# Two layer norms taken by token tiles, weight and bias applied with the copies out of PSUM, and a product moved beside the second norm

## What is computed

```python
x = _layernorm(DEEPNORM_ALPHA * x + h, ln_g[i, 0], ln_b[i, 0])      # h: GDN mixer
h = _hier_moe(x, moe_w_group[i], ..., moe_w_down[i])                # 32 experts, hidden 256
x = _layernorm(DEEPNORM_ALPHA * x + h, ln_g[i, 1], ln_b[i, 1])
x = x + jax.nn.sigmoid(x @ pe_w_gate[i]) * (p[i] @ pe_w_proj[i])

def _layernorm(t, g, b):
    mu = jnp.mean(t, axis=-1, keepdims=True)
    var = jnp.mean(jnp.square(t - mu), axis=-1, keepdims=True)
    return (t - mu) * lax.rsqrt(var + LN_EPS) * g + b
```

## Time and profile before

| what | value |
|---|---|
| median of three runs | 1308.56 us |
| profiled execution, its own time | 1311.29 us |
| its span | 1309.8 us |
| busy: PE, DVE, ACT, POOL | 1123.8, 370.3, 363.0, 48.8 us |
| mean granted TensorE clock | 0.907 of full |
| HBM read | 207.91 MB, 160 GB/s over the span |
| chain that ended last | PE 72%, SP queue 10%, DVE 6%, ACT 5%, DMA 4% |

### The profile page before, as it was taken

How to read it: one execution, slowest core, us unless ns; L and a number is a source line. 1 busy time by engine, 2 the same in 40 slices (tenths; PEclk the granted TensorE clock), 3 DMA queues, 4 the chain that set the end, 5 groups by cost and what they waited for, 6 DMA issues and landing times.

```text
span 1309.8 us, 23489 instructions
## 1 busy us (share of the span) xinstructions
PE 1123.8 (86%) x10332; PEld 852.1 (65%) x10332; DVE 370.3 (28%) x879; ACT 363.0 (28%) x902; POOL 48.8 (4%) x55
## 2 busy tenths in 40 slices
PE   6799999999889869767775979999997989996668
PEld 5577777777667654233332868888886877864457
DVE  1455655565442231000003124220002000614310
ACT  2345554655543111000003031120014011225220
POOL 1110010000000000000000000000000000400000
PEclk9799999999989969888886969999998998997559
DMA  5421221122011689999994224434441354430000
GB/s 209 185 100 66 91 75 67 67 92 74 35 66 65 280 367 407 420 421 421 422 421 193 97 100 146 159 111 147 161 160 65 101 189 115 177 129 1 0 1 33
DMA packets 35529, 210.55 MB, mean 161 GB/s; under 512 B 4688, under 2 KB 9168, under 8 KB 11488
## 3 DMA queue, kind: packets, MB, share of 16 engines
q1 hardware_dynamic: 35424, 209.00, 41.6%
HBM read 207.91 MB, written 1.08 MB: 160 GB/s over the span
## 4 chain that ended last, share of the span: by engine, by line
PE 72%; SPq 10%; DVE 6%; ACT 5%; DMA 4%; issue 2%; PEld 0%; PEldq 0%; ACTq 0%; DVEq 0%
PE ps L245 15%; SPq L230 10%; PE ps L397 10%; PE ps L1894 8%; PE ps L1812 4%; PE ps L400 4%; PE ps L698 2%; PE ps L709 2%; DMA arena<-in_wu 2%; PE ps L460 2%; PE ps L2225 2%; PE ps L426 2%; PE ps L445 2%; PE ps L261 1%; PE ps L1375 1%
## 5 line engine op out<-in xcount | busy, mean ns | idle before, releaser
L245 PE MATMUL ps<-slots,xt 128*128 128x256 f32 x640 | 139.1, 379 | 0.7 <-ACT xt L272 0.7
L397 PE MATMUL ps<-xt,slots 128*128 128x256 f32 x512 | 132.5, 407 | 2.0 <-DMA slots<-in_wu 2.0
L245 PEld LDWEIGHTS ps<-slots,xt 128*128 128x128 f32 x640 | 121.4, 190 | 17.8 <-ACT xt L272 1.1
L397 PEld LDWEIGHTS ps<-xt,slots 128*128 128x128 f32 x512 | 99.3, 202 | 26.7 <-issue 10.3
L1894 PE MATMUL ps<-slots,xt 128*128 128x256 f32 x512 | 110.7, 379 | 0.0
L1894 PEld LDWEIGHTS ps<-slots,xt 128*128 128x128 f32 x512 | 97.2, 190 | 13.2
L1375 PE MATMUL ps<-arena 128*32 128x512 f32 x304 | 48.9, 696 | 17.7 <-DMA arena<-in_wu 10.6
L400 PE MATMUL ps<-slots,arena 128*128 128x256 f32 x256 | 63.1, 389 | 0.0
L245 PE MATMUL ps<-slots,yt 128*128 128x256 f32 x256 | 57.8, 390 | 0.9 <-ACT yt L275 0.9
L1812 PE MATMUL ps<-xt,slots 128*128 128x256 f32 x256 | 58.1, 391 | 0.0
L989 DVE SCALAR_TENSOR_TENSOR arena<-arena 128x256 f32<-128x256 f32 x128 | 56.7, 489 | 0.3
(11 more groups left out here) (353 smaller groups left out, 1592.0 us busy)
## 6 DMA issues: line engine op xcount, KB each, us to landing
slots<-in_wu SPq DMA_DIRECT2D x120, 1024.0 KB, 4.9
arena<-in_wu SPq DMA_DIRECT2D x56, 1024.0 KB, 26.5
yt<-in_wu SPq DMA_DIRECT2D x10, 1024.0 KB, 26.2
arena<-bias_rows SPq DMA_DIRECT2D x1, 2048.0 KB, 15.6
arena<-in_xp SPq DMA_DIRECT2D x2, 512.0 KB, 4.4
xt<-in_xt SPq DMA_DIRECT2D x2, 512.0 KB, 9.2
x<-in_x SPq DMA_DIRECT2D x1, 1024.0 KB, 17.1
arena<-in_ln_g SPq DMA_DIRECT2D x2, 512.0 KB, 14.6
```

Source lines behind the costliest of these rows:

```text
L245: q = M.matmul(self.bank(cg, UC, t * UC), lhs[:, h * KT + k, t * P:(t + 1) * P], self.slot(s)[:, k, :], start=(t == 0 and k == 0 and h == ...
L397: q = M.matmul(bank(n, T), self.slots[:, s, k, n * P:(n + 1) * P], self.xt[:, k, :], start=(k == 0), stop=(k == KT - 1))
```

## The change

The change does five things. (1) Both norms go token tile by token tile: statistics, rsqrt, then x becomes (x - mean) * rsqrt in one DVE instruction (`norm_centre`), PE turns that (`norm_tensor`), and weight and bias are applied per feature with the copies out of the banks, four of 128x128 by ACT and four by DVE, from a small array `lnf` with features on the partitions. x itself gets its weight and bias rows afterwards (`norm_rows`). (2) In the first norm, tile 0's transposes stand ahead of the last group of the output projection, and tile 1's between the router's products of the two tiles. (3) At the end, p's product stands right behind the branch, ahead of the second norm's transposes, in banks 0 to 3; the gate projection uses banks 4 to 7. `pt` and `lnf` are loaded at the start of the MoE stage, and slot 4 is refilled ahead of slots 0 to 3. (4) The count `spill_over` of the case without spill is raised by POOL. (5) ACT's dummy Ln activations are replaced by an explicit load of the table set that holds Ln and Exp.

```diff
-        for cg in range(4):
-            self.out_rest(1, cg, 0, KT)
...
         with self.nc.Else():
-            self.nc.tensor.sem_inc(g.spill_over.sem, 1)
+            self.nc.gpsimd.sem_inc(g.spill_over.sem, 1)
+        self.moe_end_tensor(g)
+        self.moe_end_scalar(g)
         self.moe_end_vector(g)
...
     def moe_sync(self, g):
+        SP.dma_start(g.lnf, I["lnf"]).then_inc(*g.loaded.up())
+        SP.dma_start(g.pt[:, :, :], I["pt"]).then_inc(*g.loaded.up())
...
-        SP.wait_ge(*g.normed(1))
+        SP.wait_ge(*g.normed(2))
...
-        for s in range(6):
+        for s in (4, 0, 1, 2, 3, 5):
             self.fill(s, U_PE + s)
     def moe_tensor(self, g):
-        M.wait_ge(*g.normed(1))
-        self.turn_tensor(self.x, KT, [0, 1], g.turned, g.xt_kept)
-        M.wait_ge(*g.xt_kept(4))
-        M.wait_ge(*g.loaded(4))
-        for t in range(NT):
+        for cg in range(3):
+            self.out_rest(1, cg, 0, KT)
+        self.norm_tensor(g, 0, 0, OUT_BANKS[0:2])
+        self.out_rest(1, 3, 0, KT)
+        M.wait_ge(*g.loaded(6))
+        for t in range(NT):
+            M.wait_ge(*g.xt_kept(t + 1))
+            M.wait_ge(*g.xt_kept_v(t + 1))
             for k in range(KT):
                 q = M.matmul(bank(2, NG, t * NG), self.xt[:, k, t * P:(t + 1) * P], g.wr[:, k, :], ...)
+            if t == 0:
+                self.norm_tensor(g, 0, 1, OUT_BANKS[2:4])
...
     def moe_scalar(self, g):
-        A.activation(self.warm[:, 0:1], self.col(3), ACT.Ln)
-        self.norm_scalar(g, g.stats, g.var(1), 0)
-        self.turn_scalar(self.xt, KT, [0, 1], g.turned, g.xt_kept)
+        A.preload_act_table_set("natural_log_exp_and_others")
+        for t in range(NT):
+            self.norm_scalar(g, 0, t)
+            self.norm_kept_scalar(g, 0, t, OUT_BANKS[2 * t])
...
+    def norm_tensor(self, g, row, t, banks):
+        M.wait_ge(*g.centred(2 * row + t + 1))
+        for j in range(2):
+            for k in range(4):
+                q = M.transpose(self.bank(banks[j], P, k * P), self.x[:, t, (4 * j + k) * P:(4 * j + k + 1) * P],
+                                self.c["ident"])
+            q.then_inc(*g.turned.up())
+    def norm_kept_scalar(self, g, row, t, bank):
+        A.wait_ge(*g.loaded(6))
+        A.wait_ge(*g.turned(2 * (2 * row + t) + 1))
+        for k in range(4):
+            q = A.activation(self.xt[:, k, t * P:(t + 1) * P], self.bank(bank, P, k * P), ACT.Identity,
+                             scale=g.lnf[:, row, 0, k:k + 1], bias=g.lnf[:, row, 1, k:k + 1])
+        q.then_inc(*g.xt_kept.up())
+    def norm_kept_vector(self, g, row, t, bank):
+        V.wait_ge(*g.loaded(6))
+        V.wait_ge(*g.turned(2 * (2 * row + t) + 2))
+        for k in range(4, KT):
+            q = V.tensor_scalar(self.xt[:, k, t * P:(t + 1) * P], self.bank(bank, P, (k - 4) * P),
+                                g.lnf[:, row, 0, k:k + 1], g.lnf[:, row, 1, k:k + 1], ALU.mult, ALU.add)
+        q.then_inc(*g.xt_kept_v.up())
+    def norm_stats(self, g, t):    # two bn_stats of 512, one bn_aggr
+    def norm_centre(self, g, row, t):
+        V.wait_ge(*g.var_exp(2 * row + t + 1))
+        V.tensor_scalar(x, x, st[:, t, 12:13], st[:, t, 13:14], ALU.subtract, ALU.mult).then_inc(*g.centred.up())
+    def norm_rows(self, g, row, t):
+        V.wait_ge(*g.loaded(6 + 2 * row))
+        V.wait_ge(*g.turned(2 * (2 * row + t) + 2))
+        V.tensor_tensor(x, x, g.rows[:, 0], ALU.mult).then_inc(*g.step.up())
+        V.wait_ge(*g.step.last())
+        V.tensor_tensor(x, x, g.rows[:, 1], ALU.add).then_inc(*g.normed.up())
...
     def moe_vector(self, g):        # per tile t, behind the two adds of L1497
-        V.wait_ge(*g.x_added(4))
-        self.norm_vector(g, 0, g.var)
+            V.wait_ge(*g.x_added.last())
+            self.norm_stats(g, t)
+            self.norm_centre(g, 0, t)
+            self.norm_kept_vector(g, 0, t, OUT_BANKS[2 * t + 1])
+            self.norm_rows(g, 0, t)
...
+    def moe_end_tensor(self, g):
+        M.wait_ge(*g.loaded(6))
+        M.wait_ge(*self.arrived[4](self.multiplied[4].n + 1))
+        for cg in range(4): ...     # p's product, into banks 0 to 3
+        for t in range(NT):
+            self.norm_tensor(g, 1, t, (4 + 2 * t, 5 + 2 * t))
+        for t in range(NT):
+            M.wait_ge(*g.xt_kept(NT + t + 1))
+            M.wait_ge(*g.xt_kept_v(NT + t + 1))
+    def moe_end_scalar(self, g):
+        self.nc.scalar.preload_act_table_set("natural_log_exp_and_others")
+        for t in range(NT):
+            self.norm_scalar(g, 1, t)
+        for t in range(NT):
+            self.norm_kept_scalar(g, 1, t, 4 + 2 * t)
     def moe_end_vector(self, g):
+        add(0)
+        self.norm_stats(g, 0)
+        add(1)
+        self.norm_centre(g, 1, 0)
+        self.norm_stats(g, 1)
+        self.norm_kept_vector(g, 1, 0, 5)
+        self.norm_centre(g, 1, 1)
+        self.norm_kept_vector(g, 1, 1, 7)
+        for t in range(NT):
+            self.norm_rows(g, 1, t)
...
     def embed_sync(self, g):
-        SP.wait_ge(*self.normed(2))
-        SP.dma_start(g.pt[:, :, :], self.ins["pt"]).then_inc(*g.loaded.up())
     def embed_tensor(self, g):
-        M.wait_ge(*self.normed(2))
-        self.turn_tensor(self.x, KT, [0, 1], g.turned, g.xt_kept)
-        ...                         # p's product, into banks 4 to 7
-        g.projected = self.project(self.xt, 4, 1)
+        g.projected = self.project(self.xt, 4, 1, base=4)
     def embed_scalar(self, g):
-        A.activation(self.warm[:, 2:3], self.col(3), ACT.Ln)
-        self.turn_scalar(self.xt, KT, [0, 1], g.turned, g.xt_kept)
     def embed_vector(self, g):
+            if cg == 0:
+                V.wait_ge(*self.normed(4))
```

More of the change, by code:

```diff
@@ L230, in fill, with project @@
         SP.dma_start(self.slot(slot), self.ins["wu"][unit]).then_inc(*self.arrived[slot].up())
-    def project(self, lhs, units, halves, emptied=None, slots=(0, 1, 2, 3)):
+    def project(self, lhs, units, halves, emptied=None, slots=(0, 1, 2, 3), base=0):
         M, groups, done = self.nc.tensor, 4 // halves, []
@@ L1250, in moe @@
         g.og, g.cr = al("og", [P, D]), al("cr", [P, NT, 1])
+        g.pt, g.lnf = al("pt", [P, 2, T]), al("lnf", [P, 2, 2, KT])
         assert self.top <= ARENA - (NSLOT - 8) * KT * UC
@@ L1443, in moe_scalar @@
             A.activation(g.og[:, 0:512], self.bank(0), ACT.Copy).then_inc(*g.og_a.up())
[L1444 to L1449, removed]
+    def norm_tensor(self, g, row, t, banks):
+        M = self.nc.tensor
+        M.wait_ge(*g.centred(2 * row + t + 1))
[4 more added lines that the diff above has]
+            q.then_inc(*g.turned.up())
@@ L1460, in norm_vector @@
         q.then_inc(*g.step.up())
         V.wait_ge(*g.step.last())
[L1462 to L1470, removed]
-        V.wait_ge(*g.step.last())
-        V.wait_ge(*g.var_exp(row + 1))
@@ L1473, in norm_vector @@
[L1473 to L1476, removed]
+        V.bn_aggr(st[:, t, 12:14], st[:, t, 0:12]).then_inc(*g.var.up())
+    def norm_centre(self, g, row, t):
+        V, st, x = self.nc.vector, g.stats, self.x[:, t]
+        V.wait_ge(*g.var_exp(2 * row + t + 1))
+        V.tensor_scalar(x, x, st[:, t, 12:13], st[:, t, 13:14], ALU.subtract, ALU.mult).then_inc(*g.centred.up())
@@ L1645, in spill_vector @@
             q.then_inc(*g.spill_made.up())
+    def moe_end_tensor(self, g):
+        M, wp = self.nc.tensor, self.flat(4).rearrange("p (f n) -> p f n", f=2)
+        M.wait_ge(*g.loaded(6))
+        M.wait_ge(*self.arrived[4](self.multiplied[4].n + 1))
+        for cg in range(4):
+            for t in range(NT):
+                for f in range(2):
+                    q = M.matmul(self.bank(cg, UC, t * UC), g.pt[:, f, t * P:(t + 1) * P],
+                                 wp[:, f, cg * UC:(cg + 1) * UC], start=(f == 0), stop=(f == 1),
+                                 skip_group_check=True)
+        q.then_inc(*self.multiplied[4].up())
+        g.embedded = self.multiplied[4].last()
+        for t in range(NT):
[9 more added lines that the diff above has]
+            self.norm_kept_scalar(g, 1, t, 4 + 2 * t)
     def moe_end_vector(self, g):
@@ L1681, in embed_tensor @@
     def embed_tensor(self, g):
-        M = self.nc.tensor
-        M.wait_ge(*self.normed(2))
-        self.turn_tensor(self.x, KT, [0, 1], g.turned, g.xt_kept)
-        M.wait_ge(*g.xt_kept(4))
-        M.wait_ge(*g.loaded(1))
-        M.wait_ge(*self.arrived[4](self.multiplied[4].n + 1))
-        wp = self.slots[:, 4].rearrange("p a b -> p (a b)").rearrange("p (f n) -> p f n", f=2)
-        for cg in range(4):
-            for t in range(NT):
-                for f in range(2):
-                    q = M.matmul(self.bank(4 + cg, UC, t * UC), g.pt[:, f, t * P:(t + 1) * P],
-                                 wp[:, f, cg * UC:(cg + 1) * UC], start=(f == 0), stop=(f == 1),
-                                 skip_group_check=True)
-        q.then_inc(*self.multiplied[4].up())
```

(8 more changed lines are left out.)

47 lines of the change are left out of this document (25 added, 22 removed).

## The result

The kernel after took 1303.33 us (median of 5, 1300.89 to 1306.08) against 1309.36 us before (1308.28 to 1312.09): ratio 0.9948, interval 0.9929 to 0.9966, so faster by 0.3 to 0.7%. The forecast was 1294.3 with a range to 1300.4. Measured once more, beside two of the experiments, the same kernel gave 1299.51 us against 1311.82: ratio 0.9901, 0.9879 to 0.9922. The two intervals do not meet. The sign is safe, and by the two medians the size is 6 to 12 us; the forecast, 14.3 us or a ratio of 0.9891, lies outside the first interval and inside the second. That the second comes near it does not bear the forecast out: the one execution traced there, at 1303.96 us the slowest of its five, shows the same two terms missing as the first.

A forecast was written before the change was run, and what follows sets the result against it. It took two serial norms around a DMA-paced MoE stage to bound the kernel. Gains of 4.5 us (first norm) and 9.8 us (end of stage) sum to 14.3, so 1308.56 becomes 1294.3 us; 8 in 10 within 1291.3 to 1300.4.

The forecast's parts named there:

- Bounds: Whole kernel: two serial norms around a DMA-paced MoE stage; the first norm can give back idle DMA of 4.9 to 5.5 us.
- First norm: Ahead of the MoE stage: routing starts some 6 us earlier, moving the first refill from 490.96 to about 485.
- The stream: MoE weight loads: the earlier refill closes the DMA gap, 5.5 us less 0.8 for moved loads; gain taken as 4.5 us.
- The term of 4.5 us: MoE stage: the gain from closing the idle DMA stretch at the ring's refill, 4.1 to 5.2 us possible.
- rival (B): MoE refill: the first norm gives nothing, the refill still coming after the drain; 4.5 us lost, 1298.8 us, chance 0.12.
- End of the stage: Branch to gate projection: p's product behind the branch hides norm work; projection starts at 715.2 instead of 725.07, 9.8 us gained.
- Rival (A): Behind PE's branch: code arrives late, one more stall moves PE by up to 6.05 us; 1300.3 us, chance 0.15.
- Rival (C): Norms on ACT: Ln and Exp still swap tables despite the explicit load, 1.28 us each; 1295.7 us, chance 0.05.
- From there all is as before, shifted: From the gate projection on: nothing changes but the start time; no further gain or loss.
- what would show the forecast wrong: Signs: gap in PE's rows at p's product, idle DMA at refill, table load, DVE releasing tile 0's transposes, low-clock projection.

The follow-up runs named there:

- e1: The kernel after with the branch, end of the stage and embedding of before, so only the first norm is new; ratio 0.9984, -2.1 us.
- e6: The kernel after with p's product split around tile 1's transposes, tile 0's transposes ahead of it and tile 0's centring ahead of tile 1's add; ratio 0.9883.
- e8: The kernel after with the count of the case without spill raised by PE again; ratio 0.9914.
- e9: The kernel after measured again, unchanged; 1299.51 us against 1311.82 before, ratio 0.9901.
- e10: The kernel after with the old order of refills, slots 0 to 3 ahead of slot 4; ratio 0.9925.
- e4: The kernel after with one more wait on SP, before unit 18 until the second norm's rows have landed, so the DMA engines run empty once; ratio 0.9950.
- e5: The kernel after with `pt` and the second norm's two rows loaded behind the last MoE unit; ratio 0.9926.
- e7: The kernel after with the edits of e5 and e6 together; 1295.45 us against 1312.47 before, ratio 0.9876.
- e2: The kernel before with the end of after, the first norm being that of before; ratio 0.9950, -6.6 us.

## Why the prediction was wrong, point by point

**Bounds: right.** The norms were serial stretches around a DMA-paced stage, and the gap at the refill was what the first norm could reach.

**First norm: right in mechanism.** Refill 5.9 us earlier where 6 were forecast (4.2 to 4.3 in five others), gap closed, share 1.0. The median engine's landing moved by 244.3 - 240.0 = 4.3 us in after and by 3.4 to 3.8 in the five other runs with the new first norm and the rows ahead of the refill (e1, e6, e8, e9, e10); the forecast was 4.5.

**The stream: the step that failed.** It says that a fill issued at 485 "closes the gap with 1.2 us to spare. Gain: 5.5 - 0.8 = 4.7 ... I take 4.5", and it takes bytes moved for a unit landed. PE waits for a unit's last landing. The prediction had the ring and the rows landed "at about 487 us"; the last landing of the second row stands at 433.1 + 55.9 = 489.0. From there to the first refilled unit's last landing are 6.6 us, of which one unit takes 2.5, so the slowest engine stood idle for 4.1 us, not 5.5. And in after that engine is 3.9 us later with the second row (59.9), where the forecast had put 0.8 for the moved loads: the sixteen landings were already 4.9 us apart there, in place of 2.0. What is left is 0.2 us, and that is what the awaited landing moved by, for behind the refill the stream took 182.3 to 183.0 us, last landing to last landing, in all thirteen profiles. In e9, e8, e6, e1 and e10, with landings 2.9 to 4.2 us apart at the second row, the awaited one moved by 1.4 to 2.8.

The term of 4.5 us was worth -0.5 us at the scatter's end of the profiled execution (264.4 to 264.9), and 0.4 to 2.8 in the others; the rest of the loss is PE's product behind the awaited unit, which took 4.96 to 6.5 us with the clock it met. It is neither rival (B), whose gap would not have closed, nor a loss in bandwidth. e4 shows it: 5.9 us of refill given back, 0.5 us paid (1.8 against e9). Why the engines lie 3 to 5 us apart so early in the stage in these profiles and 1.9 to 2.8 in the five that kept the idle stretch stays open: e4 has the loads of after there and 2.5.

**End of the stage: right, 1.7 us too small.** PE's branch, p's product cold, transposes, copies, centring and transposes came in that order and DVE's adds started ahead (694.98). Forecast 17.6 us from the scatter's end to the projection, measured 19.3 and, on the second profile, 17.8: p's product took 10.05 where 9.1 was set (8.63 in e9), PE was back 3.3 us behind the scatter's end where 3.0 were set, and DVE's copies of four took 1.4 and ACT's 1.5 where 1.3 was set. The centring, taken at 0.75, took 0.81 to 0.83. Rival (A), a second stall behind the branch, did not occur: PE's 32 records start 3.27 us behind the scatter and run without a pause. Rival (C) didn't either, no table load stands between L1470 and L1472.

**"From there all is as before, shifted": wrong.** PE's pauses between the two groups of transposes and the projection (2.26 and 1.74 us) were followed by a low clock in the projection: 0.59 and 0.56 in the stretches from 714 to 718. From its start to `c_pool` it took 31.7 us in place of 30.0, and 32.8 in e9. I had listed this under what would show the forecast wrong and gave it no price. All seven profiles with these pauses have 31.5 to 32.8 us, all six without have 30.0, and e6 turns one into the other.

**The sum of the profiled pair.** The span fell by 6.0: -3.1 ahead of the stage, +0.5 to the scatter's end, -8.1 to the projection, +1.8 to `c_pool`, and from there +2.9 to the end. The first and the last belong to nothing that was changed: the stage's first load stands anywhere from 428.5 to 433.1 in the thirteen profiles, and the stretch from the odd stage's first loads to the end (counted from `rel_bias`) is 233.7 to 233.8 us in three of them, before among them, and 236.9 to 237.7 in the other ten. Without them the change gives 321.7 - 316.0 = 5.8 us by after's profile, 7.2 by e9's, 9.3 by e8's and e10's, where 14.3 were forecast. The range should have held this: its upper end stood on cases (A) and (B) and had no case for a term of the sum that is right in bytes and wrong in arrival.

## What to carry to other kernels

Where a full stream of DMAs feeds an engine, price a gain by the last landing of what is awaited, not by the bytes moved: the slowest DMA engine's idle time is shorter than the mean's, and an idle stretch also puts the engines back in step, so closing it can give little. Look then for data that can leave the stream, and check first on which side of the refill the wait is, for moving the rows was worth nothing while PE was late, and moving them with `pt` brought the landing 1.5 to 4.0 us forward once data were. And where a product is moved beside a norm, cut it so that it also fills PE's pauses; in these runs the pauses cost a second time, 1.5 to 2.8 us in the clock of what followed.

## What the runs showed of the hardware that was not expected

- In the six runs whose stream hardly pauses (after, e1, e6, e8, e9, e10) the sixteen landings of the awaited 1 MB unit lie 3.2 to 6.5 us apart. The distance stays the same from unit to unit over long stretches and changes in steps. In after it went from 5.0 to 6.5 us in one step near 655 us, 225 us into the stage, and the last fills took 17.05 us to issue in place of the 15.48 of before. Steps of 1.1 to 1.7 us stand at the same place, 220 to 225 us into the stage, in e1, e5, e6, e7, e8 and e9, but in none of the five runs with an idle stretch of 3 us or more, and not in e10. The DMA view of after has, in 650 to 655 us, one packet on another queue, 1.4% of 16 engines in 5 us, so about 1.1 us on one engine:

```profile
q8 instruction: 1, 0.02, 1.4%
```

Every trace has such a packet within 645 to 660 us, those without a step too. So the packet fits the step in time, but it does not by itself put the last engine further behind; what does stays open.

- A branch cost PE 6.05 us between its rows, and its next matmul started 3.1 to 3.4 us behind its last one's end in the six runs in which p's product stands first and nothing else held it (after, e2, e4, e5, e8, e9), whether PE raised the count (e8, 3.4) or not. In e6 and e7 that matmul waited for DVE, 4.4 us. ACT's and DVE's branches were hidden.

- The trace agrees with what the Trainium skill, "DMA: Bandwidth & Descriptors", section "Why a DMA increments its semaphore by 16 and not by 1", says of a transfer being split over up to sixteen engines: there are sixteen landings for each unit. What that does to a stream is the first point above.
